# Layer 2 experts as plain fp32 matmuls on two 64-column tiles, in place of three hi/lo passes

## The reference, cut to what matters

```python
def swiglu(t, wg, wu, wd):
    return (jax.nn.silu(t @ wg) * (t @ wu)) @ wd
...
    def expert_block(args):
        tok_b, w_b, e = args
        yb = swiglu(t_pad[tok_b], w_gate[e], w_up[e], w_down[e])
        return yb.astype(f32) * w_b[:, None]
```

## Time and profile before

| | us |
|---|---|
| median of 3 runs (2560.56 to 2563.84) | 2561.04 |
| span of the profiled execution, first to last instruction | 2559.4 |
| median beyond that span | 1.6 |
| TensorE busy | 2280.5 (89%) |
| VectorE busy | 1540.2 (60%) |
| ScalarE busy | 1115.6 (44%) |

### The profile page before, as it was taken

One profiled execution on the slowest core, in us unless ns is written; L12 is line 12 of the kernel. 1 busy time (PEld: TensorE's weight loads), 2 busy tenths in 40 slices (PEclk: granted clock), 3 DMA queues, 4 the chain that ended last, 5 costly groups with the idle time before them and its releaser, 6 DMA issues. The chain is left out here.

```text
span 2559.4 us, 36432 instructions
## 1 busy us (share of the span) xinstructions
PE 2280.5 (89%) x9769; PEld 1398.8 (55%) x9770; DVE 1540.2 (60%) x2716; ACT 1115.6 (44%) x1755; POOL 346.7 (14%) x335
## 2 busy tenths in 40 slices
PE   8989999879999999999956955287999999999994
PEld 1129884557777777777726911134555555555552
DVE  0134563267777777777755669714666666666664
ACT  1002451125555555555503589302555555555551
POOL 0000000011111111111101022201111111111110
PEclk9999998789999999999978977597999999999998
DMA  9962002428898999989683110324888889989874
GB/s 361 395 212 68 1 1 82 169 76 307 334 345 332 329 337 343 344 337 341 248 296 104 62 26 1 92 66 170 289 310 312 306 303 319 317 302 314 309 267 173
DMA packets 135879, 595.12 MB, mean 233 GB/s; under 512 B 32312, under 2 KB 50808, under 8 KB 78848
## 3 DMA queue, kind: packets, MB, share of 16 engines
q1 hardware_dynamic: 103600, 532.33, 57.7%
q0 software_dynamic: 31344, 53.59, 5.7%
q10 hardware_dynamic: 880, 8.49, 0.8%
HBM read 593.95 MB, written 56.20 MB: 254 GB/s over the span
## 5 line engine op out<-in xcount | busy, mean ns | idle before, releaser
L1358 DVE TENSOR_TENSOR m_w_lo<-m_wgu,m_w_hi 128x1024 fp32r<-128x1024 f32 x528 | 637.2, 1224 | 296.6 <-ACT m_w_hi L1282 280.5
L1282 ACT ACTIVATE m_w_hi<-m_wgu 128x1024 fp32r<-128x1024 f32 x528 | 548.3, 1056 | 349.6 <-PE ps L1239 185.7
L1224 PE MATMUL ps<-m_wd,m_hidT 128*128 128x512 f32 (+1 forms) x1056 | 478.3, 595 | 0.8 <-ACT m_hidT L1306 0.8
L1239 PE MATMUL ps<-m_w_hi,m_x_hi 128*128 128x512 f32 (+1 forms) x1056 | 425.4, 403 | 13.2 <-DVE m_x_lo L1350 12.7
L1239 PE MATMUL ps<-m_w_hi,m_x_lo 128*128 128x512 f32 (+1 forms) x1056 | 416.6, 395 | 0.0
L1239 PE MATMUL ps<-m_w_lo,m_x_hi 128*128 128x512 f32 (+1 forms) x1056 | 415.8, 394 | 0.0
L1165 POOL DMA_INDIRECT y_rows<-h,m_sidx x132 | 129.4, 980 | 1126.4 <-DVE h L1366 1085.8
L1224 PEld LDWEIGHTS ps<-m_wd,m_hidT 128*128 128x128 f32 (+1 forms) x1056 | 162.1, 163 | 215.7 <-issue 210.8
L1289 ACT ACTIVATE h<-ps 128x512 f32<-128x512 f32 (+1 forms) x132 | 78.5, 594 | 319.9 <-PE ps L1224 319.9
L1239 PEld LDWEIGHTS ps<-m_w_hi,m_x_hi 128*128 128x128 f32 (+1 forms) x1056 | 171.5, 162 | 79.5 <-issue 15.1
L1239 PEld LDWEIGHTS ps<-m_w_lo,m_x_hi 128*128 128x128 f32 (+1 forms) x1056 | 171.3, 162 | 73.0 <-issue 1.4
(11 more groups left out here) (264 smaller groups left out, 2841.0 us busy)
## 6 DMA issues: line engine op xcount, KB each, us to landing
m_wgu<-in_moe_w_gate SPq DMA_DIRECT2D x132, 1024.0 KB
m_wgu<-in_moe_w_up SPq DMA_DIRECT2D x132, 1024.0 KB
m_wd<-in_moe_w_down SPq DMA_DIRECT2D x132, 1024.0 KB, 4.8
ada_wbuf<-in_ada_w SPq DMA_DIRECT2D x32, 1536.0 KB, 8.2
c_rows<-y_rows SPq DMA_DIRECT2D x12, 2048.0 KB, 15.9
mods<-in_lru_w_in SPq DMA_DIRECT2D x7, 1280.0 KB, 6.9
lo_w<-in_lru_w_out SPq DMA_DIRECT2D x8, 640.0 KB, 13.9
ao_w<-in_attn_w_o SPq DMA_DIRECT2D x4, 1024.0 KB, 7.9
```

The source lines that it names most:

```text
L1224: last = pe.matmul(g.ps[0:S, YB + n, :], hidT[:, j, :], wd[:, q, j, n * 512:(n + 1) * 512], start=(j == 0), stop=(j == KF - 1))
L1239: last = pe.matmul(g.ps[0:S, GU, :].rearrange("p (a f) -> p a f", a=2), x[:, q, k, :], w[:, :, k, :], start=(k == 0 and n == 0), stop=(k = ...
L1282: act.activation(w_hi[:, :, k, :], wgu[:, q, :, k, :], ACT.Copy).then_inc(hi_s, 1)
L1358: dve.tensor_tensor(w_lo[:, :, k, :], wgu[:, q, :, k, :], w_hi[:, :, k, :].bitcast(F32), ALU.subtract).then_inc(lo_s, 1)
```

## The change

Layer 2 calls a new function, `tiled_expert_phase`; layer 1 keeps `expert_phase`.

- The split of weights and tokens into high and low parts is gone (w_hi, w_lo, x_hi, x_lo). The matmuls read `wgu` and a copy `xT` of the turned tokens as plain fp32.
- Gate and up: the 8 chunks are shared between two tiles of 64 array columns. Chunks 0 to 3 go to partitions 0 to 63 of the PSUM bank, chunks 4 to 7 to partitions 64 to 127; the instructions alternate. ScalarE copies the upper half to SBUF (`upper`) and VectorE adds the two (`gu`), then SiLU and product follow.
- Down: output columns 0 to 511 go to partitions 0 to 63 and 512 to 1023 to partitions 64 to 127 of one bank.
- TensorE's order in a step is now gate and up of b, transposes of the hidden rows of b-1, transposes of the tokens of b+1, slots, down of b-1. Gate and up have two PSUM banks.
- A wgu buffer is free when the gate and up matmuls of its block are done (`gu_done`), no longer when its split is done.

```diff
-                    sp.wait_ge(lo_s, CHUNKS * b - CHUNKS)
+                    sp.wait_ge(gu_done, b - 1)
...
-                        for k in range(KC * c, KC * (c + 1)):
-                            for n, (x, w) in enumerate(((x_hi, w_hi), (x_lo, w_hi), (x_hi, w_lo))):
-                                last = pe.matmul(g.ps[0:S, GU, :].rearrange("p (a f) -> p a f", a=2), x[:, q, k, :],
-                                                 w[:, :, k, :], start=(k == 0 and n == 0), stop=(k == KD - 1 and n == 2))
+                    for k in range(KH):
+                        for half in range(2):
+                            kk = half * KH + k
+                            last = pe.matmul(g.ps[half * S:(half + 1) * S, GU + q, :].rearrange("p (a f) -> p a f", a=2),
+                                             xT[:, q, kk, :], wgu[:, q, :, kk, :], start=(k == 0), stop=(k == KH - 1))
+                    last.then_inc(gu_done, 1)
...
+                    for j in range(KF):
+                        for half in range(2):
+                            last = pe.matmul(g.ps[half * S:(half + 1) * S, YB, :], hidT[:, j, :], wd[:, q, j, half * H:(half + 1) * H],
+                                             start=(j == 0), stop=(j == KF - 1))
+                    last.then_inc(y_done, 1)
...
+                def step(i, q):
+                    b = 2 * i + q
+                    peeled = isinstance(i, int) and i == 0
+                    gate_up(i, q, early=peeled)
+                    if not (peeled and q == 0):
+                        turn_hidden(i - 1 + q, 1 - q, first=peeled)
+                    turn_tokens(i + q, 1 - q)
+                    slots(i + 1 + q, 1 - q)
+                    if not (peeled and q == 0):
+                        down(i - 1 + q, 1 - q, early=(isinstance(i, int) and 2 * i + q == 1))
...
+                    act.activation(upper[:], g.ps[S:2 * S, GU + q, :], ACT.Copy).then_inc(upper_s, 1)
...
+                    dve.tensor_tensor(gu[:], g.ps[0:S, GU + q, :], upper[:], ALU.add).then_inc(gu_s, 1)
...
-                expert_phase(g, 1, LAT_TILES, routes, weights)
+                tiled_expert_phase(g, 1, LAT_TILES, routes, weights)
```

269 lines of the change are left out of this document (added).

## The result

| | before | after |
|---|---|---|
| median (lowest to highest), us | 2562.44 (2560.56 to 2564.58) | 2412.99 (2411.05 to 2416.70) |
| ratio, 95% interval | | 0.9418 (0.9405 to 0.9432) |
| profiled execution's span | 2559.4 | 2414.9 |

The change takes 149 us off, 5.8%. The forecast was 2407.5; it is 5.5 us, 0.2%, too low. The profiled execution is the longest of the four (2416.70), so times read from its trace lie some 4 us above those of a median one.

The account below looks back on a forecast made before the run. TensorE was taken to bound the layer 2 expert phase, DMA next. A step of 8.8 us put the combine's read at 1798 + 64 x 8.8 = 2361, 153.5 us earlier, giving 2407.5 us, range 2355 to 2530.

Parts of the forecast that it names:

- The bound: Layer 2 expert phase before the change: TensorE bounds its 10.98 us step, with DMA the next limit at 3.41 MB a block.
- The overlap of tiles: Layer 2 gate, up and down matmuls run on both column tiles at once; TensorE's step 8.07 to 9.7 us, chance 0.65.
- full overlap: All but first and last record paired across tiles: gate and up 4.05 us, down 2.29, TensorE's step 8.07.
- estimated step of 8.4 us: TensorE's layer 2 step if two tiles give 1.59 times one tile's speed, derived from the skill's three-tile figure.
- DMA's term: Layer 2 transfers per block: 8.1 us at 420 GB/s or 9.35 at 365; leaning to 8.5 with token rows.
- T: Length of one layer 2 step after the change, the larger of TensorE's and DMA's times, taken as 8.8 us.
- jostling: TensorE (8.1 to 9.7 us) and DMA (8.1 to 9.35) are close and disturb each other, so the step is 8.8.
- Start and end: Around the 64 refilled layer 2 blocks: first refill at 1781.9, 2 us to first data, 14 us tail before the combine.
- What costs nothing: Added ScalarE copy (0.59 us) and VectorE add (0.68) per layer 2 block are covered by the next step, 8 us later.
- Tiles that don't overlap: Rival: layer 2 matmuls run one after the other, step 12.35 us, 2646 us, slower than before; chance 0.19.
- The clock: Rival: TensorE idles for weights each layer 2 step, its clock falls to 0.74, step 10.2 us, 2497 us; chance 0.12.
- The gather as a chain: Rival: scatter, gather, transposes and down chain over two layer 2 steps, 13.7 us; binds over 12; at worst 2440, inside main case.

## Why the prediction was right, and where its terms were off

**The bound.** Right. TensorE bounded the step and DMA was next; half the bytes take 107 us from the changed kernel, so DMA bounds it now, with the share at 1.00.

**The overlap of tiles.** Right in kind, mis-sized. The prediction's full overlap had "16 records take 9 slots" and "8 take 5", a pair being tile A's low record beside tile B's high one. The trace has both tiles start at once: 8 slots and 4. In the run with half of the loads, where TensorE hardly waits, gate and up are 3.62 us instead of 4.05, down 1.77 instead of 2.29, and the transposes and slots 1.41 for 1.73. TensorE's step is 6.80, not 8.07.

The Trainium skill (TensorE: Matmul & The Clock Gate, Part 3) gave, by its three column tiles at 79% of ideal, an estimated step of 8.4 us. The trace has two tiles at 1.93 times one (7.03 to 3.65 us), 96% of ideal. The same part of the Trainium skill says that matmuls start strictly in program order. The run with tile A's chunks first disagrees: tile B's first four records ran beside tile A's last four.

**DMA's term.** Here the sum was off, and T came out better than its parts. The prediction's 8.1 us at 420 GB/s is 7.5 for the weights (3.146 MB) and 0.6 for the bytes of the token rows; "with about 0.4 us for the token rows" it gave them 1.0. Weights alone are 7.50 us (both rows left out, 418 GB/s, the rate of the earlier trace rows's first stretch), gather 1.06, scatter 0.36: 8.92, and 8.93 was measured. So the weights were priced right and the token rows 0.4 us too low, because of the gather. T = 8.8 added 0.3 for jostling between two terms that were thought close. With TensorE at 6.80 they are not, and no run shows such a term; that it covered most of the gather's missing cost was luck. The queue never ran dry, as predicted, but at a share of 1.00 it moves 379 GB/s and not 420. The second stretch of the earlier trace rows, 365 GB/s at a share of 1.00 with gather and scatter between, had shown such a rate.

T was 0.13 too small, 64 x 0.13 = 8 us in the profiled execution: the combine reads at 2369.27 where 1798 + 64 x 8.93 gives 2369.5 and the prediction had 2361. The median lies 3.7 us below that execution, which leaves the miss of 5.5.

The Trainium skill (DMA: Bandwidth & Descriptors, Bandwidth) has 425 GB/s for a transfer of 16 MB issued from GpSimd. The 418 of the kernel without token rows, in loads of 1 MB issued from SP, lies 2% below it.

**Start and end.** The first refill was put at 1781.9 and came at 1782.25, by two errors against each other. The first gate and up began at 1776.67 and not at 1774.2, as the expert phase began some 2.5 us later in this execution. They took 5.3 us, not 7.7: 8 slots and not 9, and only the first four at the low clock (the weight loads are 0.86 us apart up to 1780.09 and 0.43 behind it).

**What costs nothing.** Right. The copy of the upper half (593 ns) and the add (682 ns) have a whole step to hide in, and VectorE and ScalarE are at 33% and 23%.

**The rivals.** Tiles that don't overlap: the run on one tile is that rival, 2621 us where 2646 was worked out, as its step is 11.94 and not 12.35: transposes and slots take 0.2 less, gate and up and down 0.1 less each. The clock: TensorE waits, and now and then the clock falls to the lower level (mean 0.95), but the slow blocks fit into time that DMA leaves (its share stays at 1.00), so it costs nothing that shows. The prediction's "no gap is over about a microsecond" was wrong (longest 3.8), since weights come late in bursts. The gather as a chain: late twice in 50 blocks, by 0.4 us at most, so it is not the chain, as predicted, though its transfer costs in another way, by the queue.

## What to carry to other kernels

When the engine that bounds a loop gets faster, price the next resource from what shares it, term by term: here a small gather cost three times its bytes in DMA time, and an allowance made for another reason hid it. A plain fp32 product with 64 output rows wants both column tiles; on one tile it loses to three fp32r passes. Once transfers bound a loop, one gain left is to use a queue that idles before it. The run with two blocks ahead suggests giving these blocks buffers whose release lets the next fetch start; that was not run.

## What the runs showed of the hardware that was not expected

- Two column tiles run plain fp32 matmuls in full parallel: 16 records in 8 slots of 0.43 us.
- A matmul for the other tile can start ahead of three records that come before it in the program: 12 slots and not 15 with tile A's chunks first.
- Token rows read into the core slow the weight packets beside them, by 0.56 us in 7.6 a block; rows written out do not. Neither indexed access (some 0.13 us of 1.06) nor the half of the partitions that takes the rows explains it.
- After one wait of 3.8 us TensorE's granted clock is 0.52 in the stretch behind it, and gate and up take 5.35 instead of 3.65 us.
